# Two-part transformer kernel on one Trainium2 core: query and key units in one pass of 512 columns, and a new order of work at several places

## What is computed

```
def _mixer(h, w_in, conv_w, w_conv_out, w_attn_out, w_o, rel_bias):
    u = h @ w_in
    q, k, v, cb, cc, ch, g_conv, g_attn = jnp.split(u, splits, axis=-1)
    y_conv = (cb * _causal_dwconv(cc * ch, conv_w)) @ w_conv_out
    ...
    logits = jnp.einsum("bnqrhe,bnkrhe->bnrhqk", qb, kb).astype(jnp.float32) * (HEAD_DIM ** -0.5)
    logits = jnp.where(mask, logits + bias, NEG_INF)
    ...
    merged = jax.nn.sigmoid(g_conv) * y_conv + jax.nn.sigmoid(g_attn) * y_attn
    return merged @ w_o
```

```
    xr = causal_conv(xr, conv_w[l], conv_b[l])
    hr = rg_lru(xr, rg_a_w[l], rg_a_b[l], rg_x_w[l], rg_x_b[l], lru_lambda[l])
    y_a = (hr * jax.nn.gelu(xg)) @ w_lru_out[l]
```

## Time and profile before

| | |
|---|---|
| median of three runs | 2119.05 us |
| the profiled execution's own time | 2119.83 us |
| its span, first to last instruction | 2118.0 us |
| TensorE matmul busy | 2065.3 us (98%) |
| VectorE busy | 1419.6 us (67%) |
| ScalarE busy | 1031.6 us (49%) |
| DMA | 438 MB, 207 GB/s over the span |
| granted TensorE clock, mean | 0.996 |

### The profile page before, as it was taken

One profiled execution on the slowest core, in us unless ns is written; L12 is line 12 of the kernel. 1 busy time (PEld: TensorE's weight loads), 2 busy tenths in 40 slices (PEclk: granted clock), 3 DMA queues, 4 the chain that ended last, 5 costly groups with the idle time before them and its releaser, 6 DMA issues.

```text
span 2118.0 us, 29720 instructions
## 1 busy us (share of the span) xinstructions
PE 2065.3 (98%) x12033; PEld 1811.1 (86%) x12033; DVE 1419.6 (67%) x1801; ACT 1031.6 (49%) x1278; POOL 36.5 (2%) x78
## 2 busy tenths in 40 slices
PE   6999999999999999999999999999999899899998
PEld 6788899999888878888999998887788788897887
DVE  5787677668777777767766786555555577656454
ACT  3543544444544363445454446444644569646443
POOL 0000000000000000000000000000000000000000
PEclk9999999999999999999999999999999999999999
DMA  9787698547687758758865585554656434456552
GB/s 298 251 272 250 199 298 253 130 133 253 229 267 251 249 170 285 243 195 270 280 173 142 176 291 194 194 179 150 227 180 195 131 126 134 158 181 203 187 196 80
DMA packets 355933, 438.11 MB, mean 207 GB/s; under 512 B 9571, under 2 KB 323371, under 8 KB 355796
## 3 DMA queue, kind: packets, MB, share of 16 engines
q1 hardware_dynamic: 350592, 420.51, 60.8%
q0 software_dynamic: 4160, 14.23, 3.1%
q10 hardware_dynamic: 1044, 1.46, 0.2%
HBM read 435.05 MB, written 1.11 MB: 206 GB/s over the span
## 4 chain that ended last, share of the span: by engine, by line
PE 84%; DVE 6%; ACT 5%; DMA 2%; issue 2%; DVEq 1%; SPq 0%; ACTq 0%
PE PC L1781 7%; PE PC L1783 7%; PE PC L1782 7%; PE PA L1781 6%; PE PA L1783 6%; PE PA L1782 6%; PE PB L1781 5%; PE PB L1783 5%; PE PB L1782 5%; PE PA L1774 5%; PE PA L1775 5%; PE PA L1776 5%; PE PC L1774 2%; PE PC L1776 2%; PE PC L1775 2%; DVE acc L1196 2%
## 5 line engine op out<-in xcount | busy, mean ns | idle before, releaser
L1170 DVE TENSOR_TENSOR lo<-raw,hi 128x2048 fp32r<-128x2048 f32 x275 | 628.8, 2289 | 229.7 <-ACT hi L697 229.1
L697 ACT ACTIVATE hi<-raw 128x2048 fp32r<-128x2048 f32 x277 | 529.0, 1911 | 264.0 <-PE PC L1783 130.3
L1774 PE MATMUL PA<-nl,hi 128*128 128x256 f32 x976 | 281.5, 288 | 1.0 <-ACT f L1090 0.9
L1775 PE MATMUL PA<-nh,lo 128*128 128x256 f32 x976 | 276.0, 283 | 0.0
L1776 PE MATMUL PA<-nh,hi 128*128 128x256 f32 x976 | 275.9, 283 | 0.0
L1196 DVE SCALAR_TENSOR_TENSOR acc<-raw,cs,acc 128x256 f32<-128x256 f32 x448 | 217.1, 485 | 34.0 <-issue 0.4
L1781 PE MATMUL PA<-hi,nl 128*128 128x512 f32 (+1 forms) x528 | 210.8, 399 | 10.7 <-DVE nl L1272 7.6
L1783 PE MATMUL PA<-hi,nh 128*128 128x512 f32 (+1 forms) x528 | 206.4, 391 | 0.0
L1782 PE MATMUL PA<-lo,nh 128*128 128x512 f32 (+1 forms) x528 | 205.9, 390 | 0.0
L1774 PEld LDWEIGHTS PA<-nl,hi 128*128 128x128 f32 x976 | 187.0, 192 | 2.8 <-issue 1.1
L1775 PEld LDWEIGHTS PA<-nh,lo 128*128 128x128 f32 x976 | 187.0, 192 | 0.3
(11 more groups left out here) (305 smaller groups left out, 3867.2 us busy)
## 6 DMA issues: line engine op xcount, KB each, us to landing
raw<-in_w_in SPq DMA_DIRECT2D x90, 1024.0 KB, 6.4
raw<-in_ada_w SPq DMA_DIRECT2D x66, 1024.0 KB, 7.2
raw<-in_ffn_w_gate SPq DMA_DIRECT2D x88, 512.0 KB, 4.1
raw<-in_ffn_w_up SPq DMA_DIRECT2D x88, 512.0 KB, 5.1
raw<-in_ffn_w_down SPq DMA_DIRECT2D x44, 1024.0 KB, 5.0
raw<-in_ffn_w SPq DMA_DIRECT2D x88, 512.0 KB, 4.8
raw<-in_ffn_w SPq DMA_DIRECT2D x22, 1024.0 KB, 4.9
raw<-in_w_o SPq DMA_DIRECT2D x12, 1024.0 KB, 6.3
```

The costliest lines, as they stand in the source:

```text
L697: A(parts_of(n)[0], raw[:, n % 3, :], ACT.Copy).then_inc(hi_done, 1)
L1170: V.tensor_tensor(l, raw[:, n % 3, :], h.bitcast(F32), ALU.subtract).then_inc(lo_done, 1)
L1774: MM(o, wh[:, c0:c0 + w], xl, start=first, stop=False, skip_group_check=True)
L1775: MM(o, wl[:, c0:c0 + w], xh, start=False, stop=False, skip_group_check=True)
```

## The change

- **Queries and keys.** `nh` and `nl` become the two halves of one tensor `nn`. `unit_both` multiplies a weight block's high part with both in one matmul of 512 columns, and its low part with `nh` in one of 256: 32 matmuls for 48. The results lie side by side in two banks of PSUM; ScalarE copies one of the two (now unscaled), and VectorE adds the other (24 new instructions, twelve a mixer, each ahead of a `split`). The factor 1/8 moves into VectorE's sum of logits and bias. TensorE's first attention step of a mixer waits for the twelfth of these additions (`qk_done`).
- **Last mixer.** On VectorE the last two taps go behind the attention's step of i = 1, `lru(j - 1, 2)` behind that of i = 2 and `lru(j - 1, 3)` to i = 4. On ScalarE `gelu(j)` goes from i = 4 to i = 5 behind the exponentials, the high part (`lru(j - 1, 2)`) from i = 1 to i = 3.
- **Opening.** `normed(0, 0)` and `turn_x(0, 0)` come one ada product earlier, `normed(0, 1)` and `turn_x(0, 1)` before the first products of stage 0.
- **Changes.** Ahead of s = 7 ScalarE computes the norm's sums of token tile 0 before both of the post-norm of tile 1. Ahead of s = 6 and 8 both engines split the fourth unit before the norm's sums. In the feed-forwards' first step VectorE writes the hidden low part before the split.

```diff
-        nh = sb("nh", [P, KC, T], F32R)
-        nl = sb("nl", [P, KC, T], F32R)
+        nn = sb("nn", [P, 2, KC, T], F32R)
+        nl, nh = nn[:, 0, :, :], nn[:, 1, :, :]
...
+        both = [PA[:, :], PC[:, 0:1024], PC[:, 1024:2048]]
...
                 elif s == 6:
                     row_std(*post_of(s, 0))
-                    row_first(*post_of(s, 1))
                     next_stats(s, 0)
-                    row_second(*post_of(s, 1))
+                    row_std(*post_of(s, 1))
...
                     split(BASE[s + 1] + 2)
+                    split(BASE[s + 1] + 3)
                     next_stats(s, 0)
...
                     after(b + 6 + n)
-                    if n % 2:
-                        A(o, prod[n % 3], ACT.Copy)
-                    else:
-                        A(o, prod[n % 3], ACT.Copy, scale=HD ** -0.5)
+                    A((k1 if n % 2 else q1)[:, n // 2 * 2:n // 2 * 2 + 2, :],
+                      both[n % 3].rearrange("p (c e t) -> p c e t", c=2, e=2)[:, :, 1, :], ACT.Copy).then_inc(qa_done, 1)
                     split(b + 9 + n)
...
+                if i == 5 and 0 <= j < 4:
+                    gelu(j)
                 if i == 3 and j >= 0:
                     recurrent_gates(j)
+                if i == 3 and 1 <= j < 4:
+                    lru(j - 1, 2)
...
                 if i == 4 and 0 <= j < 4:
                     lru(j, 0)
-                    gelu(j)
...
-                    split(b + 3 * i + 2)
+                    if i > 1:
+                        split(b + 3 * i + 2)
                     low(i - 1)
+                    if i == 1:
+                        split(b + 3 * i + 2)
...
-                        V.tensor_tensor(L, SC[:, 0:pr * w].rearrange("p (g n) -> p g n", g=pr),
-                                        b[:, :, ::-1] if w == 256 else b[:, :, 127::-1], ALU.add)
+                        V.scalar_tensor_tensor(L, SC[:, 0:pr * w].rearrange("p (g n) -> p g n", g=pr), HD ** -0.5,
+                                               b[:, :, ::-1] if w == 256 else b[:, :, 127::-1], ALU.mult, ALU.add)
...
-                if n == 4:
+                if n == 3:
                     normed(0, 0)
                 dve.wait_ge(raw_full[u] if u < 4 else ada_in[u - 4], 16)
                 ada_unit(u * UC, first_ada(u), ada_d)
+            normed(0, 1)
             mods(0)
...
+                    if n >= 6:
+                        dve.wait_ge(qa_done, l * 12 + n - 5)
+                        o = (k1 if n % 2 else q1)[:, (n - 6) // 2 * 2:(n - 6) // 2 * 2 + 2, :]
+                        V.tensor_tensor(o, both[n % 3].rearrange("p (c e t) -> p c e t", c=2, e=2)[:, :, 0, :], o,
+                                        ALU.add).then_inc(qk_done, 1)
                     split(b + n + 3)
...
+                if i == 1 and 0 <= j < 4:
+                    taps2(j, (2, 3))
+                if i == 4 and 1 <= j < 4:
+                    lru(j - 1, 3)
+                    dve.drain()
...
-                if i == 1 and j >= 1:
+                if i == 2 and 1 <= j < 4 or i == 1 and j == 4:
                     lru(j - 1, 2)
...
-                if i == 2 and 1 <= j < 4:
-                    lru(j - 1, 3)
...
+            def unit_both(n, o):
+
+                arrive(n)
+                wh, wl = parts_of(n)
+                for m in range(2):
+                    for kk in range(KC):
+                        c = slice(kk * UC + m * P, kk * UC + (m + 1) * P)
+                        MM(o[:, m * 512:(m + 1) * 512].rearrange("p (e t) -> p e t", e=2), wh[:, c], nn[:, :, kk, :],
+                           start=kk == 0, stop=False, skip_group_check=True)
+                        i = MM(o[:, m * 512:m * 512 + T], wl[:, c], nh[:, kk, :], start=False, stop=kk == KC - 1,
+                               skip_group_check=True)
                 i.then_inc(unit_done, 1)
...
-                up(0, 1, 0, s, lambda: turn_x(s, 1))
+                up(0, 1, 0, s, (lambda: turn_x(s, 1)) if s else None)
...
-                    unit(b + 6 + n, prod[n % 3], nh, nl)
+                    unit_both(b + 6 + n, both[n % 3])
...
+                        if j == 0 and u == 0:
+                            pe.wait_ge(qk_done, 12 * (l + 1))
                         tick(1, st0, 4 * j, 2 * u, v1, l * 4 + j if j else None)
```

More of the change, by code:

```diff
@@ L195, in squared @@
 def squared(s, t, h):
-    if (s, t) == (6, 1):
-        return 3 * STAT[("p", 6, 0)] + 3 + (6 if h else 1)
     return 3 * STAT[("p", s, t)] + (3 if h else 1)
@@ L411, in build @@
         gb_full, gate_mm, gate_rdy, fin_full = sem("gb_full"), sem("gate_mm"), sem("gate_rdy"), sem("fin_full")
-        v_done = sem("v_done")
+        v_done, qa_done, qk_done = sem("v_done"), sem("qa_done"), sem("qk_done")
         b_full = [sem(f"b_full{i}") for i in range(2)]
@@ L857, in hidden_tile @@
                     A(by_tile(hid(cH, i))[:, t], turned(i)[:, t], ACT.Copy).then_inc(hH_done, 1)
-                split(b + 3)
+                if s - 1 not in BARE:
+                    split(b + 3)
                 silu(0, 0)
@@ L1002, in mixer @@
                     after(b + 6 + n)
-                    o = (k1 if n % 2 else q1)[:, n // 2 * 2:n // 2 * 2 + 2, :].rearrange("p c t -> p (c t)")
-                    if n % 2:
-                        A(o, prod[n % 3], ACT.Copy)
-                    else:
-                        A(o, prod[n % 3], ACT.Copy, scale=HD ** -0.5)
+                    A((k1 if n % 2 else q1)[:, n // 2 * 2:n // 2 * 2 + 2, :],
+                      both[n % 3].rearrange("p (c e t) -> p c e t", c=2, e=2)[:, :, 1, :], ACT.Copy).then_inc(qa_done, 1)
                     split(b + 9 + n)
@@ L1096, in recurrent_gates @@
                 if j:
-                    act.wait_ge(lru_v, 6 * j)
+                    act.wait_ge(lru_v, 6 * j - 1)
                 for m in range(2):
@@ L1148, in _ @@
                     split(b + 6 + u)
-                if i == 1 and j >= 1:
+                if i == 1 and j == 4:
                     lru(j - 1, 2)
@@ L1538, in _ @@
             split(1)
-            normed(0, 1)
+            dve.drain()
             apply(0, 1)
@@ L1722, in conv2, with taps2 @@
                                     ALU.mult, ALU.add)
-                for tap in (1, 2, 3):
+                taps2(j, (1,))
+            def taps2(j, taps):
+                for tap in taps:
                     dve.drain()
@@ L1728, in conv2 @@
                                                    vec[:, c:c + 1], xc[:, m * T:(m + 1) * T], ALU.mult, ALU.add)
-                i.then_inc(xc_done, 1)
+                if taps[-1] == 3:
+                    i.then_inc(xc_done, 1)
             for hu in range(2 * len(SPREAD)):
@@ L1802, in unit @@
                     i = half(n, o, m, xh, xl, nk, cw)
+                i.then_inc(unit_done, 1)
+            def unit_both(n, o):
[8 more added lines that the diff above has]
+                               skip_group_check=True)
                 i.then_inc(unit_done, 1)
@@ L2056, in _ @@
             i.then_inc(mod_done, 1)
+            turn_x(0, 1)
             def bias_lines():
```

## The result

| | before | changed |
|---|---|---|
| median | 2119.21 us (4 runs, 2118.66 to 2120.47) | 2097.97 us (4 runs, 2097.69 to 2099.45) |
| the profiled execution's own time | 2119.83 us | 2099.45 us |
| its span | 2118.0 us | 2097.4 us |

The ratio is 0.990, 95% interval 0.9883 to 0.9917: 21.2 us faster where 17 were forecast, 2097.97 for 2102 and inside the range. The page's line of busy times, against the earlier trace rows: 384 matmuls fewer, VectorE 13 us more, ScalarE 3 instructions fewer (the table loads).

The account below looks back on a forecast made before the run. TensorE was taken as the bound, its matmuls filling 2065.3 of 2118.0 us. Terms 3.4 - 4.9 - 2.6 - 2.6 - 1.3 - 9 = -17 take 2119.83 to 2102.8, median 2102 us; range 2097 to 2107.

Parts of the forecast that it names:

- step 7: Last mixer: moving taps, scan and gelu with its table load ends three waits recurring three times; -9 us.
- step 2: Query and key units, VectorE: additions make a split late, TensorE waits 3.35 us; +3.4 us over both mixers, saving included.
- 1: Query and key units, TensorE: wide plus narrow matmul saves 13 ns over three narrow; 5.1 us over 24 units.
- Rival one: Query and key units: VectorE keeps up because ada weights come sooner; -5.1 instead of +3.4, 2093.5 us; chance 0.17.
- 3: Opening: turns of x move into TensorE's waits, the ada vector comes at 38.5; -4.9 us.
- 4: Feed-forwards' first step, stages 2 and 3: writing cL before the split ends waits of 1.3 us each; -2.6 us.
- term 5: Ahead of stages 6 and 8: splitting the fourth unit earlier ends two waits for f; -2.6 us.
- 6: Change from stage 6 to 7: tile 0's sums first, recip earlier, wait for xn_a from 2.4 to 0.9; -1.3 us.

Follow-up runs that it names:

- experiment 4: Changed kernel with the eight wide matmuls first, then the eight narrow ones, in each output block instead of in turn; 2099.7 us (0.9905).
- experiment 2: Changed kernel without VectorE's 24 additions, the attention's first step waiting for ScalarE's copies instead; 2094.58 us (0.9884).
- experiment 1: Changed kernel with the query and key units as before: 48 matmuls of 256 columns, scaled copy, no additions; 2100.19 us (0.9912).
- experiment 12: Changed kernel with the fourth split for stages 6 and 8 and the norm's sums ahead of stage 7 in their old places; 2103.58 us (0.9926).
- experiment 7: Changed kernel with the last mixer's gelu ahead of the high part's write and the exponentials again; 2102.33 us (0.9921).
- experiment 9: Changed kernel with the last mixer as before except that two taps stay behind the attention's step; 2109.39 us (0.9952).
- experiment 3: Changed kernel with high and low part side by side for each contraction step, so the wide matmul's operand is one piece; 2098.07 us (0.9898).
- experiments 4 and 6: The latter: changed kernel with the last mixer's scan and neighbours one half-unit earlier again, ScalarE's high part with it; 2108.49 us (0.9952).

## Why the prediction was right, and where it was not

The range held because the terms' signs and the large term's size were right; that the large term's size was right is in part luck, as step 7 shows. The miss of 3.6 us inside the range comes mostly from step 2. By its steps:

**1, wrong in size.** "One wide and one narrow matmul ... save 13 ns": the pair takes 353 ns for three narrow ones' 360, so 7 ns, 0.11 us a unit (copies 5.65 us apart, not 5.55) and 2.7 us at most instead of 5.1. The distance of 512-column matmuls came from a stream of their own kind; in turn with narrow ones it is 4 ns more (experiment 4). By the Trainium skill, TensorE: Matmul & The Clock Gate, section Back-to-back issue gap (N / 2.4 + 2.5 ns for an isolated matmul), an estimate of the saving is 2.5; the 7 measured lie between that and my rows, and the distances of experiment 4, 230 and 119 ns, are 14 and 10 over the page's.

**2, mechanism right, size wrong.** VectorE is late for the tenth unit, and experiment 2 shows that its additions are why. The wait was 1.17 and 1.44 us, not 3.35. The step that failed is the carry of "0.42" and "1.22 more" through the ada products. VectorE's timeline of the changed kernel:

```profile
289.31 0.35 DVE L1194 TENSOR_SCALAR acc<-raw,cs 128x256 f32<-128x256 f32 x1 [2.33 <-DMA raw<-in_ada_w]
...
299.09 0.35 DVE L1194 TENSOR_SCALAR acc<-raw,cs 128x256 f32<-128x256 f32 x1
...
319.41 0.35 DVE L1194 TENSOR_SCALAR acc<-raw,cs 128x256 f32<-128x256 f32 x1 [2.34 <-DMA raw<-in_ada_w]
...
324.80 0.68 DVE L1583 TENSOR_TENSOR q<-PA,q 128x512 f32<-128x512 f32 x1
325.39 2.28 DVE L1171 TENSOR_TENSOR lo<-raw,hi 128x2048 fp32r<-128x2048 f32 x1
```

Less the lead of 4.45 us, the product at 299.09 is at 303.54, 0.65 sooner than in the earlier trace rows, though two additions stand ahead of it: the one before it had started 0.95 sooner, on weights that landed sooner. The product at 319.41 is at 323.86, 0.15 late. With the sixth addition the split is 0.75 late, not 2.15. I had taken the landing as fixed to the request, 5.5 us from the end of one product to the start of the next ahead of the gate's sums. In both mixers it is 5.0 to 5.3 there in all twelve profiled kernels with wide matmuls, also without the additions (experiment 2), and 5.4 to 6.5 in the two with narrow ones (before, experiment 1). So it is not chance between executions alone; which part of the change moves it no run shows. (The prediction also names this split the second of its pair; it is the first.) The wait for the twelfth addition, put at 0.7 and 1.25, did not show: with the chain not late, it is done in time. Rival one had this premise right, that the weights come sooner, against my argument that at a DMA share of 1.03 they can't; its -5.1 was wrong too: even with VectorE out of the way (experiment 2) the two mixers were only 3.2 us shorter than before, up to the same row.

**3, right.** The ada vector (`modt`) came at 38.81, 3.2 us sooner, for 38.5 forecast; the rest, to -4.45, is `turn_x(0, 1)`.

**4, right in stages 2 and 3** (-1.24 and -1.09 for -1.3 each), though as the sum of two things (5), and it is worth 0.7 each in stages 6 and 8, where I had counted nothing: there term 5 pays out in full (1.7 each for 1.0) only because this edit stands behind it.

**5, too small.** I put a stop at its idle time (1.3). Each costs 1.7 to 1.8 (experiment 12). Part of it is the start behind the stop: the four turns of `f` take 0.59 us to the next product in the kernel before (1497.49 to 1498.08) and 0.36 in the changed one. Stages 2 and 3 gave only 1.1 to 1.2, but not because their stops were cheap. TensorE's turns of `f` are 18.41 us apart across the stop in the kernel before and 16.81 in the changed one, so the stop of 1.31 cost 1.60 here too (1.57 in stage 3). But the next two turns, 16.8 apart before, are now 17.13 apart (17.23 in stage 3): TensorE comes to the next step 1.6 us sooner, VectorE's `cL` there does not (it starts 33.1 us from the stage's head, 32.4 before), and in stage 3 TensorE stands 0.17 us for it (at 801.55). Before:

```profile
590.18 0.60 PE L1870 MATMUL PA<-ident,f 128*128 128x128 f32 x4
...
608.59 0.60 PE L1870 MATMUL PB<-ident,f 128*128 128x128 f32 x4
```

Changed:

```profile
586.00 0.60 PE L1904 MATMUL PA<-ident,f 128*128 128x128 f32 x4
...
602.81 0.60 PE L1904 MATMUL PB<-ident,f 128*128 128x128 f32 x4
...
619.94 0.60 PE L1904 MATMUL PA<-ident,f 128*128 128x128 f32 x4
```

**6, right:** `recip` at 1658.63, 9.6 us ahead of before, 8.1 of it won earlier, so 1.5 by the edit; the wait for `xn_a` 0.89.

**7, right in its sum, wrong in its reasons.** "Each is longer than the wait that it caused" failed. Nine waits went, and the stretch is 9.2 us shorter; but the taps' move brought nothing, and two of the three waits a cycle were one lateness of ScalarE, ahead of a split and the exponential, that went with the gelu. That the sum came out is luck in so far as all three were moved together. Had the change moved the taps and the scan alone, my reasoning would have promised at least the waits for `otok` and `negm`, 6.6 us, and the chip given 5.7 (experiment 7); had it moved the taps alone, 4.3 (the rival of experiment 9), and the chip gave nothing. The one microsecond put down to the mixer's end was exchanged: the wait for `oL` of 0.56 went, the one for `cL` stayed, and one for a split's low part came (1.43, at 1811.90).

## What to carry to other kernels

A wait names its last releaser, not its cause: before moving work away from ahead of it, follow that engine back past its last idle row, since a table load on ScalarE can show up as a late maximum on VectorE. On an engine that is over 90% busy in a stretch, a saving elsewhere that costs it instructions is given back at the first place where that engine is last; ask first which of its instructions could go into an idle gap of its own. And a stop is not worth exactly its idle time: four of 1.3 us cost 1.6 to 1.8 here, and in two places the move that ended one made the next step 0.3 to 0.4 late, so count from start to start, and past the next step.

## What was unexpected of the hardware

Mostly the clock. The stretch from the second wait of the opening (47.78) to stage 1 holds the same instructions in all the kernels with the new opening, but took 199.5 us in the profiled execution of the changed kernel, 197.9 in that of experiment 1 and 201.1 in that of 9. The stretch table (us, TensorE busy, granted clock, DMA share, GB/s) of the changed kernel and of experiment 1:

```profile
48.00:52.00 4.00, 4.00 (x12) 0.57 0.99 358
```

```profile
48.00:52.00 4.00, 4.00 (x19) 1.00 1.00 373
```

A granted clock of 0.57 means that most of these four microseconds ran at 1.2 GHz, behind a stop of 1.75 us; in experiment 1, behind a stop of 0.92, all of them ran at 2.4. Of twelve profiled executions with the new opening the four with a stop under 1.2 us took 197.9 to 198.0, seven with one from 1.3 to 2.05 took 199.5 or more, and one with 1.66 us (experiment 3) took 197.9, so the stop alone does not decide. Stops of 2.2 to 2.5 us in experiments 4 and 6 were followed by the same fall elsewhere, one of 2.02 in experiment 9 (at 1768.66) was not. The executions of one kernel mostly follow their mean granted clock: experiment 1's four took 2099.2 at 0.999, 2099.6 and 2100.8 at 0.998, and 2102.7 at 0.997. It is not all of it: two of experiment 12's, both at 0.997, are 4.2 us apart. This is one reason why kernels whose traces differ by 0.3 us elsewhere can have medians 2 us apart here.
